# Splitting the opening of a fused two-block transformer kernel into quarters of the features, with modulation slabs that hold shift and scale side by side

## The reference, cut to what matters

```python
mod = silu(c) @ ada_w + ada_b                  # [2048] @ [2048, 6144]
shift, scale, gate = split(mod, 3)             # 2048 each
h = rms_norm(x, norm_g) * (1 + scale) + shift
proj = h @ w_in                                # [256, 2048] @ [2048, 9296]
a_q, a_k, a_v, a_g, i_q, i_k, i_w, r_q, r_f, r_i, r_g = split(proj, ...)
...                                            # sparse attention, gated recurrence, w_out, gate
```

## Time and profile before

| | us |
|---|---|
| median of three runs | 2517.64 (2517.01 to 2518.13) |
| profiled execution, own time | 2518.42 |
| its span in the trace | 2516.6 |
| PE busy | 2479.7 (99%) |
| DVE busy | 1486.8 (59%) |
| ACT busy | 1150.7 (46%) |
| POOL busy | 106.1 (4%) |
| time of the first product of the projection, from the span's start | 65.03 |

### The profile page before, as it was taken

The page is one execution under the profiler, slowest core; times in us unless marked ns, Lnnn a source line. Parts: engine busy times, 40 slices in busy tenths (PEclk is TensorE's granted clock), DMA queues, the critical chain, the costliest instruction groups (busy, mean ns, idle before and its releaser), DMA issues.

```text
span 2516.6 us, 28692 instructions
## 1 busy us (share of the span) xinstructions
PE 2479.7 (99%) x11518; PEld 2058.8 (82%) x11518; DVE 1486.8 (59%) x1772; ACT 1150.7 (46%) x1484; POOL 106.1 (4%) x152
## 2 busy tenths in 40 slices
PE   6999999999999999999999999999999999999998
PEld 6888778888788888888888888888888888888887
DVE  5888889666755455454444755765654455544444
ACT  2545566444544444344343544554544444444332
POOL 0210000000100000000000212100000000000000
PEclk9999999999999999999999999999999999999999
DMA  9996555565455555556555655446556555556553
GB/s 394 349 358 231 193 201 177 175 240 178 151 185 189 195 184 190 194 184 208 193 197 188 193 194 180 162 135 205 180 189 195 185 189 195 184 192 210 191 194 134
DMA packets 186164, 507.06 MB, mean 201 GB/s; under 512 B 17792, under 2 KB 18080, under 8 KB 184752
## 3 DMA queue, kind: packets, MB, share of 16 engines
q1 hardware_dynamic: 174544, 460.07, 54.6%
q0 software_dynamic: 10960, 42.99, 4.8%
q10 hardware_dynamic: 528, 2.16, 0.2%
HBM read 503.06 MB, written 2.10 MB: 201 GB/s over the span
## 4 chain that ended last, share of the span: by engine, by line
PE 96%; DVE 2%; DMA 1%; ACT 1%; issue 0%; SPq 0%; DVEq 0%; ACTq 0%
PE acc L592 30%; PE acc L594 30%; PE acc L593 30%; DMA raw<-in_ada_w 1%; PE wk L1023 1%; PE wk L615 1%; DVE lo L1677 1%; PE acc L711 1%; PE wk L1079 0%; PE wk L1105 0%; PE wk L776 0%; ACT hi L1157 0%; DVE scale_a L1654 0%; PE wk L1066 0%; PE acc L717 0%
## 5 line engine op out<-in xcount | busy, mean ns | idle before, releaser
L592 PE MATMUL acc<-hi,h 128*128 128x512 f32 x2592 | 1021.6, 394 | 3.3 <-issue 1.8
L594 PE MATMUL acc<-hi,h 128*128 128x512 f32 x2592 | 1011.3, 390 | 0.0
L593 PE MATMUL acc<-lo,h 128*128 128x512 f32 x2592 | 1010.6, 390 | 0.0
L1677 DVE SCALAR_TENSOR_TENSOR lo<-raw,gcols,hi 128x1024 fp32r<-128x1024 f32 (+1 forms) x464 | 569.4, 1278 | 239.0 <-ACT hi L1157 236.1
L1675 DVE TENSOR_TENSOR lo<-raw,hi 128x1024 fp32r<-128x1024 f32 (+1 forms) x388 | 453.4, 1213 | 319.9 <-ACT hi L1157 319.2
L1157 ACT ACTIVATE hi<-raw,gcols 128x1024 fp32r<-128x1024 f32 (+1 forms) x464 | 495.4, 1129 | 276.8 <-PE acc L594 230.2
L592 PEld LDWEIGHTS acc<-hi,h 128*128 128x128 f32 x2592 | 487.7, 188 | 105.9 <-issue 4.5
L594 PEld LDWEIGHTS acc<-hi,h 128*128 128x128 f32 x2592 | 487.7, 188 | 102.7
L593 PEld LDWEIGHTS acc<-lo,h 128*128 128x128 f32 x2592 | 488.1, 188 | 98.5 <-issue 0.2
L1157 ACT ACTIVATE hi<-raw 128x1024 fp32r<-128x1024 f32 (+1 forms) x388 | 385.5, 1048 | 367.0 <-DMA raw<-in_w_ffn_down 229.5
L592 PE MATMUL acc<-hi,g_hi 128*128 128x512 f32 x704 | 274.2, 389 | 0.0
(11 more groups left out here) (323 smaller groups left out, 1238.7 us busy)
## 6 DMA issues: line engine op xcount, KB each, us to landing
raw<-in_w_ffn_gate SPq DMA_DIRECT2D x176, 512.0 KB, 3.8
raw<-in_w_ffn_up SPq DMA_DIRECT2D x176, 512.0 KB, 4.6
raw<-in_w_ffn_down SPq DMA_DIRECT2D x176, 512.0 KB, 4.7
raw<-in_w_in SPq DMA_DIRECT2D x144, 512.0 KB, 4.6
raw<-in_w_kv SPq DMA_DIRECT2D x64, 512.0 KB, 4.7
ada_raw<-in_ada_w POOLq DMA_DIRECT2D x32, 512.0 KB, 6.9
gate_raw<-in_ada_w POOLq DMA_DIRECT2D x32, 512.0 KB, 6.1
raw<-in_w_out SPq DMA_DIRECT2D x32, 512.0 KB, 5.1
```

The costliest lines, as they stand in the source:

```text
L592: pe.matmul(o, l_hi, w_hi[:, c], start=first, stop=False)
L593: pe.matmul(o, l_hi, w_lo[:, c], start=False, stop=False)
L594: mm = pe.matmul(o, l_lo, w_hi[:, c], start=False, stop=last)
L1677: ins = vec.scalar_tensor_tensor(out=lo[:, r, c], in0=raw[:, r, c], scalar=gcols[:, st.gain, k:k + 1], in1=hi[:, m % HI_SLOTS, c], op0=ALU ...
```

## The change

The features 0 to 1023 are opened in two quarters of 512. A modulation slab below 16 now holds, for 256 rows, 512 columns of the shift and 512 of the scale side by side, so that slabs 0 to 7 give both for the features 0 to 511 and slabs 8 to 15 for 512 to 1023. The stage `first` of six groups is replaced by `quarter1` (three groups, two slabs each, features 0 to 511), `quarter2` (the same three groups, features 512 to 1023) and a `first` for the other three groups. There are 24 slabs as before. All transposes of `xn` are parked in `xnT`, in the place of `h_lo`. PE takes two modulation slabs itself in place of four. SP issues the opening's fetches only when an earlier one has landed. In the middle of slab 5 PE sums the second quarter's columns. For the groups in `LOADED` the earlier partial result is copied by ACT from `proj` into the PSUM banks (`seg_load`), PE adds to it there, and ACT evacuates the sum. For the other groups DVE adds as before. Tables and gate slabs are moved to other slabs of the order.

```diff
-    shift_a, scale_a = at("shift_a", [P, GW], slot(8)), at("scale_a", [P, GW], slot(8) + 4)
-    ada_sum = [shift_a, scale_a, tmp1, tmp2, gate[:, 0:GW], gate[:, GW:D]]
+    ada_sum = [gate[:, 0:GW], gate[:, GW:D], tmp1, tmp2, gate[:, 0:GW], gate[:, GW:D]]
...
-    st_first = S("first", 6, 4, 2, 2, HALF, 2, wide(w_in, FIRST), h)
+    st_q1 = S("quarter1", 3, 2, 2, 2, HALF, 2, wide(w_in, FIRST), h)
+    st_q2 = S("quarter2", 3, 2, 2, 2, HALF, 2, wide(w_in, FIRST, 2), h, k0=KT // 4)
+    st_first = S("first", 3, 4, 2, 2, HALF, 2, wide(w_in, FIRST[3:]), h)
...
+    slabs = [(st, g, s) for st in (st_q1, st_q2, st_first) for g in range(st.groups) for s in range(st.slabs)]
...
-    ADA_COLS = (0, D, GW, D + GW, 2 * D, 2 * D + GW)
-    N_ADA, N_MOD, N_START, N_RING = 48, 32, 16, 12
-    PE_ADA = (2, 5, 8, 11)
...
+    ADA_COLS = (0, HALF, GW, D + GW, 2 * D, 2 * D + GW)
+    N_ADA, N_MOD, N_QUARTER, N_START = 48, 32, 8, 16
+    PE_ADA = (1, 3)
...
+    GATE_AT = (24, 25, 26, 27, 28, 30, 38, 42, 47, 49, 52, 54, 55, 66, 68, 72)
...
         gates = sum(t <= m for t in GATE_AT)
-        if m == 0:
-            return N_RING + 1
-        return N_MOD + gates if gates else min(N_START + max(0, 16 * (m - 1) // 18), N_MOD)
+        return N_MOD + gates if gates else (7, 8, 9, 11, 13, 14, 16)[m] if m < 7 else min(N_START + m - 7, N_MOD)
...
-    T_LB, T_COLS, T_TURN, T_TABLES, T_GAINS = 5, 20, 21, 23, 25
+    T_LB, T_COLS, T_TABLES, T_GAINS = 26, 22, 24, 26
...
+    LOADED = [("quarter2", 1), ("quarter2", 2), ("second", 2), ("second", 3)]
...
     def ada_part(a, part):
 
         k, c = 2 * (a % 8) + part, ADA_COLS[a // 8]
-        return ada_w[k * P:(k + 1) * P, c:c + GW], ada_slot(a)[:, part * GW:(part + 1) * GW]
+        dst = ada_slot(a)[:, part * GW:(part + 1) * GW]
+        if a >= N_START:
+            return ada_w[k * P:(k + 1) * P, c:c + GW], dst
+        both = ada_w[k * P:(k + 1) * P, 0:2 * D].rearrange("p (e n) -> p e n", e=2)
+        return both[:, :, c:c + HALF], dst.rearrange("p (e n) -> p e n", e=2)
...
+        for a in range(4):
+            if a >= 2:
+                ada_wait(sp, a - 2)
+            ada_fetch(a, raw_landed[1 + a])
+        for a in range(4, N_QUARTER - 1):
+            ada_wait(sp, a - 2)
+            ada_fetch(a, early_landed[a - 4])
...
         for m in range(N_SLABS):
             st, g, s = slabs[m]
             r = place(m) % RING
             if m == 1:
-                early(N_RING + 1, N_START)
-            if m < RING:
-                wait_summed(place(m) - RING)
-            else:
+                ada_wait(sp, 6)
+                ada_fetch(N_QUARTER - 1, early_landed[3])
+                sp.wait_ge(raw_landed[0], 32)
+            if m == 2:
+                ada_wait(sp, N_QUARTER - 1)
+                ada_fetch(8, quarter_landed[0])
+                sp.wait_ge(raw_landed[1], 64)
+            if m == 3:
+                ada_wait(sp, 8)
+                for a in (9, 10):
+                    sp.wait_ge(xn_ready, a - 8)
+                    ada_fetch(a, quarter_landed[a - 8])
+                    sp.wait_ge(raw_landed[2], 64)
+                ada_wait(sp, 9)
+            if m == 4:
+                ada_wait(sp, 10)
+                for a in (11, 12):
+                    sp.wait_ge(ada_added, added(a - 4))
+                    ada_fetch(a, early_landed[a - 9])
+                    sp.wait_ge(raw_landed[3], 64)
+                ada_wait(sp, 11)
+            if 1 <= m < RING:
+                wait_summed(m - 1)
+            elif m:
                 sp.wait_ge(slab_used, m - RING + 1)
...
-                        pe.wait_ge(mod_ready, (1, 2, 4, 4)[b])
+                        pe.wait_ge(mod_ready, (1, 1, 2, 2)[b])
+                    elif s == 0 and (st.name, g) in LOADED:
+                        pe.wait_ge(acc_loaded[b], LOADED.index((st.name, g)) + 1)
...
+                            first = first and (st.name, g) not in LOADED
...
+        def quarter_columns(block, banks, start):
+
+            pe.wait_ge(ada_added, added(8 * (block + 1)))
+            for pair in range(2):
+                for e in range(2):
+                    for f in (2 * pair, 2 * pair + 1):
+                        ins = pe.matmul(quarter_col(banks, e, f), ada_sum[block][:, e * HALF + f * P:e * HALF + (f + 1) * P],
+                                        ones[:, 0:1], start=start, stop=True, skip_group_check=not start)
+                ins.then_inc(ada_turned, 1)
...
+        pe.wait_ge(xn_ready, TT)
+        for i in range(8):
+            if i >= 4:
+                pe.wait_ge(xn_parked, i - 3)
             turn_xn(i).then_inc(turned, 1)
-        pe.wait_ge(ada_added, added(N_START))
-        for f in range(8):
-            ins = summed(1, scale_col(f), f)
-            if f in (1, 3, 7):
-                ins.then_inc(ada_turned, 1)
+        quarter_columns(0, acc, False)
...
-            product(*slabs[m])
+            if m == 5:
+                product(*slabs[m], (0,))
+                second_columns()
+                product(*slabs[m], (1,))
+            else:
+                product(*slabs[m])
...
+        def park(i):
+
+            act.wait_ge(turned, i + 1)
+            act.activation(xnT[:, :, 2 * i:2 * i + 2, :], wk[:, i % 4, :].rearrange("p (k t c) -> p t k c", k=2, t=TT), ACT.Copy
+                           ).then_inc(xn_parked, 1)
+
         for i in range(4):
-            act.activation(xnT[i], wk[:, i, :], ACT.Copy).then_inc(xn_parked, 1)
+            park(i)
         conv_to(0)
+        for i in range(4, 8):
+            park(i)
         split_modulated(0)
-        for i in (1, 2):
-            split_modulated(i)
-            conv_to(i)
-        split_modulated(3)
+        conv_to(1)
+        split_modulated(1)
+        conv_to(2)
...
+        def seg_load(st, g, seg):
+
+            for t in range(TT):
+                for n in range(2):
+                    b = st.bank(t, n)
+                    act.wait_ge(acc_free[b], use[st.name, g, b])
+                    act.activation(acc[:, b, :], proj[:, seg, t, n * HALF:(n + 1) * HALF], ACT.Copy
+                                   ).then_inc(acc_loaded[b], 1)
...
+                if st is st_q1 or (st.name, g) in LOADED:
+                    seg_evac(st, g, FIRST_SEGS[g])
                 if st is st_first:
-                    seg_evac(st, g, FIRST_SEGS[g])
+                    seg_evac(st, g, FIRST_SEGS[3 + g])
                 if st is st_small:
                     small_evac()
+                if (st.name, g + 1) in LOADED:
+                    seg_load(st, g + 1, FIRST_SEGS[g + 1])
...
+            if m in (4, T_COLS, T_COLS + 1):
+                i = 2 if m == 4 else 4 + 2 * (m - T_COLS)
+                split_modulated(i)
+                split_modulated(i + 1)
...
+        def quarter_scales(q, pair, banks):
+
+            vec.wait_ge(ada_turned, 2 * q + pair + 1)
+            c = slice(4 * q + 2 * pair, 4 * q + 2 * pair + 2)
+            vec.tensor_tensor(sh[:, c], banks[:, 2 * pair, 0:2], gcols[:, B_SHIFT, c], ALU.add)
+            for f in range(2):
+                k = 4 * q + 2 * pair + f
+                ins = vec.tensor_scalar(gs[:, k:k + 1], banks[:, 2 * pair + 1, f:f + 1], gcols[:, B_SCALE, k:k + 1],
+                                        gcols[:, N_MIX, k:k + 1], ALU.add, ALU.mult)
+            ins.then_inc(mod_ready, 1)
...
-        ada_to(7)
+        ada_to(4)
         vec.wait_ge(x0_squares, TT)
         rsqrt(rstd[:], stats[:, 0:2], D, stats[:, 4:6], stats[:, 6:8])
         vec.sem_inc(rstd0_ready, 1)
-        ada_to(13)
-        vec.wait_ge(ada_turned, 1)
-        step(vec.tensor_tensor(sh[:, 0:8], acc[:, 3, 0:8], gcols[:, B_SHIFT, 0:8], ALU.add))
+        ada_to(N_QUARTER - 1)
         conv_to(0)
-        ada_to(N_START)
-        first_scales(2, 0, 2)
-        first_scales(3, 2, 4)
-        first_scales(4, 4, 8)
+        ada_to(N_QUARTER)
+        quarter_scales(0, 0, acc)
+        quarter_scales(0, 1, acc)
         split_modulated(0)
-        for i in (1, 2):
-            conv_to(i)
-            split_modulated(i)
-        split_modulated(3)
+        conv_to(1)
+        split_modulated(1)
+        conv_to(2)
...
+            if (st is st_second or st is st_q2) and s == st.slabs - 1 and (st.name, g) not in LOADED:
...
-        for a in range(N_START, N_MOD):
-            if a < N_START + 2:
-                pool.wait_ge(early_landed[3], 32)
-            elif a == N_START + 2:
-                pool.wait_ge(ada_turned, 4)
-            else:
-                pool.wait_ge(ada_added, added(a - 2))
+        for a in range(13, N_MOD):
+            pool.wait_ge(ada_added, added(a - 4 if a < N_START else a - 2))
             for part in range(2):
                 src, dst = ada_part(a, part)
-                pool.dma_start(dst, src).then_inc(ada_landed[(a - N_START) % 3], 16)
-            if a == N_START + 2:
+                pool.dma_start(dst, src).then_inc(ada_landed[ada_ring(a)], 16)
```

185 lines of the change are left out of this document (84 added, 101 removed).

## The result

Over 20 runs each on one chip, the changed kernel takes **2522.01 us** (2518.00 to 2524.33) and the kernel before 2517.76 (2516.86 to 2520.76). The ratio is 1.0014 (95% interval 1.0008 to 1.002): slower by some 4 us, inside the 0.2% that I had set as no difference. The forecast was 2509.3. The profiled execution took 2520.04 us, 2 us under the median, its span is 2518.2, against 2516.6 in the earlier trace rows. The product is now in lines L649 to L651, `hi` L1212, `lo` L1740, the first-stage evacuation L1307, the load into PSUM L1316.

A forecast was written before the change was run, and what follows sets the result against it. PE was taken as the bound, busy 2479.7 of 2516.6 us. First product 22.2 earlier, less 7.7 and costs of 2.0, 0.3, 0.5, 1.4, 0.9, 1.0, gave 8.4 us less: 2510.0 profiled, 2509.3 median; range 2503 to 2519.

The forecast's parts named there:

- The spacing of the held-back slabs: Opening: with each fetch waiting for the slab two before it, slabs land 2.6 us apart, about as before.
- The first product: End of the opening: PE's first product starts at 42.8 us, 22.2 us earlier than before.
- The first four slabs land as before: Start of the opening: landings unchanged, slab 2 at 17.58 and slab 3 at 19.98 us.
- DVE is the bound: Second quarter: DVE's sums and conversions last until 80.9 us, PE idles 5.2 us, slab 6 starts at 86.0.
- what would show the forecast wrong: Signs: DVE waiting for transfers between 46 and 81, PE waiting for `lo`, or ACT over 10 us for a weight slab.
- The rival of a longer chain: From 42.7 to 86.0 us: DVE's chain takes 4 to 8 us more, giving 2513 to 2517; chance 0.2.
- The rival on starvation: Opening: held-back slabs 3.3 us apart, first product 1.9 us later, 2511; counted inside the forecast, no chance of its own.
- The slower rival: Until the second half's columns at slab 22, transfers bind: 2514 at 338 GB/s, 2522.7 at 317; chance 0.09.
- The clock: Behind PE's pause ahead of slab 6: restarting at the lower clock costs 2.0 us, bounds 0 and 3.0.
- The loads: `LOADED` groups: PE waits 0.3 and 0.5 us after DVE-added groups, 1.4 and 0.9 after ACT-evacuated ones.
- DVE's small losses: Behind slab 6: lateness of DVE passing to PE costs 1.0 us, bounds 0 and 4.
- A rule that the prediction weighed: ACT's loads into PSUM: a skill statement that ScalarE writes PSUM faster would make them some tenths shorter; 0.6 us was taken.

The follow-up runs named there:

- The best two runs: Changed kernel without landing waits, modulation slab 7 ahead of weight slab 0, second quarter's scales earlier, bounds and gains' products moved: 2508.97 us with PSUM loads, 2508.37 us without.
- two pairs of runs: Changed kernel with against without loads into PSUM: 2522.01 and 2520.29 us with landing waits, 2513.04 and 2511.19 us without landing waits.
- the third pair: Changed kernel without landing waits, with slab 7, scales, bounds and gains' products all moved: 2508.97 us with loads into PSUM, 2508.37 us without.
- the run with bounds and gains apart: Changed kernel without landing waits, forget gate's bounds moved from slab 26 to 12, products of rotary tables and gains from 26 to 33: 2510.73 us, ratio 0.9971.

## Why the prediction was wrong

The forecast for the profiled execution was 2510.0, measured 2520.04. Of these 10.0 us slab 6 holds 8.4 (94.4 in place of 86.0), and behind it small losses add 1.8 and clock and loads give back 0.3 each. A last 0.4 stays open, and so do the 2 us by which the median lies above the profiled execution.

- **The spacing of the held-back slabs: the step that failed.** "Unhindered, the second transfer of a slab lands 4.6 us after its issue ... so two slabs in flight bring one in 2.5 us, as now. I take 2.6." The 4.6 us come from a later stage, in which the slabs need not follow one another at full rate (187 GB/s on average behind 420 us). In the opening the same transfer takes 5.4 with two slabs in flight and the spacing is 2.9, 346 GB/s over 20 to 60 us in place of 419. With three in flight or no waits the rate is 412 and 413, and 8.5 to 9 us come back.
- **The first product** came at 45.4 in place of 42.8, and at 46.3 in three other runs with the same waits; without waits and with the same opening order it came at 44.2 to 45.0. So the waits cost 0.5 to 2 of it. The larger part is another step: "The first four slabs land as before". Slab 1 was there for PE at 15.3 (14.8 without waits), where I had some 12.4, so PE's two sums ended at 29.1 where I had 27.0. Transposes, parking, `hi` (0.66 more for weight slab 0), `lo` and DVE's slab 7 follow in series. The run with rows of 4 KB has the landing back at 12.6. From the last sum to the first product it took 5.55, forecast 5.6.
- **"DVE is the bound" in the second quarter.** Not in the changed kernel. There the bytes were, and PE stopped ahead of slab 4, which the forecast did not price. I named the sign of it among what would show the forecast wrong (DVE waiting for transfers between 46 and 81, ACT over 10 us for a weight slab), and both stand in the trace with 4.21 and 11.45. With bytes out of the way the step was right to a us: DVE's conversions end at 81.65 (forecast 80.9), slab 6 starts at 86.92 (86.0) from a first product 1.4 later, after 1.21 + 4.82 us of idle PE (0.7 + 5.2). The rival of a longer chain had 4 to 8 us more at this place, and 8.4 came, but not by its reasons: DVE's own sums and POOL's slabs were in time, and what was late came by SP's held-back queue.
- **The rival on starvation** saw the hold-back's danger and stopped it at the first product: 1.9 us. The measured price is 8.5 to 9. What it left out is that the transfers have no pause until 75 us, so that what slab 7 is late by, weight slab 4 is late by too, and more.
- **The slower rival** had the transfers as a bound, but at slab 22, and by a falling rate. That stretch was kept fed: PE has no stop between 119.33 and 222.77.
- **The clock.** 2.0 was taken for one pause. There were two, ahead of slabs 4 and 6, with 2.5 and 1.7 us lost behind them. The granted clock is 0.54 from 76 to 82 us and 0.72 from 94 to 100, and the matmuls at 76.86 and 77.28 are 0.43 us apart, the pace of the lower level of 1.2 GHz. The 0.73 of the stretch from 40 to 60 above is not one of them: there the first product begins at half pace, as it did before. The best two runs have one left, at 70.
- **The loads.** Slab 8: 0.3, measured nothing. Slab 10: 1.4, measured 1.27. The two in `second`: 0.5 + 0.9, measured 0.67 + 0.85. These terms were right. One was not priced: what the loads are worth. By two pairs of runs it is less than they cost by some 1.8 us; in the third pair 0.6 is left and not told apart from nothing.
- **DVE's small losses.** 1.0, measured 1.39 + 0.69 + 1.30 less 0.56, 2.8. By the run with bounds and gains apart, all of it goes with the two pieces of work at slab 26, the bounds (moved there from slab 5) and the gains' products (from 25), right ahead of additions that PE waits for. I had called the moved tables free.
- **A rule that the prediction weighed.** The groups of ACT by shape between 65 and 420 us have

```profile
L1307 ACT ACTIVATE proj<-acc 128x512 f32<-128x512 f32 x40 | 23.1, 595 | 28.5 <-PE acc L651 28.4
...
L1316 ACT ACTIVATE acc<-proj 128x512 f32<-128x512 f32 x16 | 9.1, 598 | 14.2 <-DVE proj L2057 14.1
```

  so copies out of PSUM and into it take the same 0.60 us, as taken, and the Trainium skill's statement ("ScalarE: Activation LUTs", Step-by-step) that PSUM is the faster destination does not show at this size. It is no clean test, since the source changes with the destination. The sum did not use it.

## What to carry to other kernels

A queue that is held back for the sake of order needs enough in flight for the time from issue to landing *at full load*: size it as landing time over the spacing wanted, from transfers in a saturated stretch, and read GB/s beside the DMA share, since the share still reads 0.99 to 1.00 when a sixth of the rate is gone. While transfers run without a pause, count bytes, not single transfers: what is lost or passed over early is paid in full at the next slab that someone waits for, and moving one slab ahead only changes who waits. And before a table or a small sum is moved "beside" the bound engine, look at what stands right behind it in its engine's program.

## What the runs showed of the hardware

- One core, 512 KB transfers from SP: 346 GB/s with two slabs (four transfers) in flight (331 in the run without loads, which has the same waits), 412 with three (six), 413 with no hold-back (11.5 us from issue to landing). No gain was measured beyond three. Rows of 4 KB in place of 2 KB moved 352 with two in flight. The Trainium skill ("HBM Reference", Specifications (TRN2)) puts a core that streams alone at about 425 GB/s; by the 418 of the kernel before the trace agrees, and the 358 that I had weighed is the share of a core whose pair streams too.
- The DMA share, which counts the time of the packets, reads 0.99 to 1.00 at 344 to 348 GB/s and 1.03 to 1.05 at 411 to 420. In four other traces with two slabs in flight it reads 0.94 to 0.96 at 322 to 338, from 20 to 40 us.
- With rows of 2 KB modulation slab 1 was there for PE at 14.6 to 15.8 us in twelve traces, with rows of 4 KB at 12.4 and 12.6 in two.
- The first product began at half pace in every trace, for 6 to 14 matmuls, and so did the products behind the column sums at 182 us and later, where PE does not stop. Behind the first product, PE went on at half pace, for 7 to 13 matmuls, after every stop of 2.4 us and more up to 120 us, and at full pace after those of 1.6 us and less. One pair is between: behind a stop of 1.2 us and the 16 one-column matmuls of the second quarter (no landing waits) it kept full pace, behind 1.5 to 1.6 us and the same 16 (the runs with no loads, with the tables apart and with three in flight) it ran 9 to 11 at half pace from 80.5 to 81.1 on. Some 1.5 to 2.7 us are lost each time. What decides was not tried.
- These losses move single traces by as much as an edit does. The run without landing waits ran 10 matmuls at half pace behind slab 6's start at 86.92, 2.1 us, the one with the tables apart none. Around the column sums it is the other way round, by 1.6 us. The verdicts above therefore rest on medians.
